# Splitting the 512-column products of the down and output projections into two of 256 columns

## The reference

```python
# first block, per layer
    x = x + jnp.einsum('bsnd,bsnd->bsd', gates, up) @ w_out[l]      # output projection, 1024 x 1024
    h = rmsnorm(x, norm_mlp_g[l])
    x = x + jnp.square(jax.nn.relu(h @ w_up[l])) @ w_down[l]        # 1024 -> 4096 -> 1024
...
# second block, per layer: two FFNs of this kind around a mixer
def _swiglu(x, w_in, w_out):
    gate, up = jnp.split(x @ w_in, 2, axis=-1)
    return (jax.nn.silu(gate) * up) @ w_out                         # 1024 -> 2 x 2816, 2816 -> 1024
...
        mixed = jnp.concatenate([o_a, o_b, o_c, o_d], axis=-1)
        h = h + g2[:, None, :] * (mixed @ w_out[l])                 # output projection, 1024 x 1024
```

## Time and profile before

| | |
|---|---|
| median of 3 runs | 2006.86 us (2004.92 to 2009.09) |
| the profiled execution | 2007.09 us, its span 2004.3 us |
| PE busy | 1952.3 us, 97% of the span, 13792 matmuls |
| PEld busy | 1761.0 us, 88%, 13792 loads |
| DVE busy | 1444.8 us, 72% |
| ACT busy | 1148.6 us, 57% |
| DMA | 409.55 MB, mean 204 GB/s |
| the chain that ended last | PE 79%, DVE 14%, ACT 5%, issue 2% |

### The profile page before, as it was taken

One profiled execution on the slowest core, in us unless ns is written; L12 is line 12 of the kernel. 1 busy time (PEld: TensorE's weight loads), 2 busy tenths in 40 slices (PEclk: granted clock), 3 DMA queues, 4 the chain that ended last, 5 costly groups with the idle time before them and its releaser, 6 DMA issues.

```text
span 2004.3 us, 33258 instructions
## 1 busy us (share of the span) xinstructions
PE 1952.3 (97%) x13792; PEld 1761.0 (88%) x13792; DVE 1444.8 (72%) x1922; ACT 1148.6 (57%) x1814; POOL 43.4 (2%) x32
## 2 busy tenths in 40 slices
PE   7999999999999999999899999999999999999999
PEld 7898888888989898888799988699989998878998
DVE  5756798888565788988756589765576657977555
ACT  6358845455436865454655566755565556566554
POOL 0100000000010000000000000000000100000000
PEclk9999999999999999999999999999999999999999
DMA  7453378996554356999455542365546554334553
GB/s 275 144 210 107 125 265 326 389 386 245 194 189 149 105 176 267 391 388 374 167 187 189 189 158 96 107 205 185 184 154 213 189 187 151 126 127 151 188 187 126
DMA packets 56164, 409.55 MB, mean 204 GB/s; under 512 B 6608, under 2 KB 6992, under 8 KB 7888
## 3 DMA queue, kind: packets, MB, share of 16 engines
q1 hardware_dynamic: 46512, 330.23, 46.5%
q10 hardware_dynamic: 9504, 77.21, 9.5%
HBM read 406.37 MB, written 1.05 MB: 203 GB/s over the span
## 4 chain that ended last, share of the span: by engine, by line
PE 79%; DVE 14%; ACT 5%; issue 2%; DMA 0%; DVEq 0%; ACTq 0%; SPq 0%
PE bank L603 25%; PE bank L605 24%; PE bank L604 24%; DVE weights_low L405 4%; ACT weights_high L383 1%; DVE work L2417 1%; DVE work L1517 1%; DVE scratch L1445 1%; ACT work L465 1%; PE bank L940 1%; DVE work L566 1%; DVE h_low L572 1%; ACT weights_high L384 0%; DVE work L1607 0%; DVE scratch L1602 0%
## 5 line engine op out<-in xcount | busy, mean ns | idle before, releaser
L405 DVE TENSOR_TENSOR weights_low<-raw_weights,weights_high 128x1024 fp32r<-128x1024 f32 x608 | 728.4, 1237 | 364.2 <-ACT weights_high L383 357.2
L603 PE MATMUL bank<-h_high,weights_high 128*128 128x256 f32 x3024 | 857.7, 284 | 15.0 <-DVE h_low L572 11.1
L605 PE MATMUL bank<-h_high,weights_low 128*128 128x256 f32 x3024 | 845.3, 280 | 0.0
L604 PE MATMUL bank<-h_low,weights_high 128*128 128x256 f32 x3024 | 844.7, 279 | 0.0
L383 ACT ACTIVATE weights_high<-raw_weights 128x1024 fp32r<-128x1024 f32 x296 | 313.4, 1059 | 619.6 <-PE bank L605 587.9
L603 PEld LDWEIGHTS bank<-h_high,weights_high 128*128 128x128 f32 x3024 | 567.9, 188 | 36.7 <-issue 17.0
L604 PEld LDWEIGHTS bank<-h_low,weights_high 128*128 128x128 f32 x3024 | 568.4, 188 | 2.9 <-issue 0.5
L605 PEld LDWEIGHTS bank<-h_high,weights_low 128*128 128x128 f32 x3024 | 568.6, 188 | 0.0
L384 ACT ACTIVATE weights_high<-raw_weights 128x1024 fp32r<-128x1024 f32 x296 | 309.0, 1044 | 0.0
L603 PE MATMUL bank<-weights_high,hidden_high 128*128 128x512 f32 x640 | 254.3, 397 | 5.1 <-DVE work L2491 2.9
L605 PE MATMUL bank<-weights_high,hidden_low 128*128 128x512 f32 x640 | 252.7, 395 | 0.0
(11 more groups left out here) (304 smaller groups left out, 1880.0 us busy)
## 6 DMA issues: line engine op xcount, KB each, us to landing
raw_weights<-in_stream SPq DMA_DIRECT2D x310, 1024.0 KB, 4.9
work<-in_ada ACTq DMA_DIRECT2D x64, 1152.0 KB, 9.4
consts<-in_consts SPq DMA_DIRECT2D x1, 2048.0 KB, 12.2
work<-in_row ACTq DMA_DIRECT2D x2, 836.0 KB, 5.5
x<-in_x SPq DMA_DIRECT2D x1, 1024.0 KB, 4.9
out_x<-x SPq DMA_DIRECT2D x4, 256.0 KB, 2.0
gain_row<-in_final SPq DMA_DIRECT2D x1, 512.0 KB, 12.8
vec<-in_vec SPq DMA_DIRECT2D x1, 169.0 KB, 12.1
```

The source lines that it names most:

```text
L405: dve.tensor_tensor(low[:, c], raw[:, c], high[:, c].bitcast(F32), ALU.subtract).then_inc(m.raw_done[plan.index[name] % RAW], 1)
L603: pe.matmul(out, aH, bH, start=start, stop=False, skip_group_check=True)
L604: pe.matmul(out, aH, bL, start=False, stop=False, skip_group_check=True)
L605: return pe.matmul(out, aL, bH, start=False, stop=stop, skip_group_check=True)
```

## The change

`three_wide` takes the place of `three` in `pe_down`, `pe_out` and `pe_mix`. It makes the three matmuls for the first 256 of the 512 columns, then the three for the other 256, with the same stationary tiles into the same bank. The flag that starts an accumulation is set on the first half alone. Every matmul loads its stationary tile as before. All waits and signals stay on the first and the last matmul of what was one triple. `T` is 256.

```diff
+def three_wide(pe, out, aH, aL, bH, bL, start, stop):
+
+    for c in (slice(0, T), slice(T, 2 * T)):
+        mm = three(pe, out[:, c], aH, aL, bH[:, c], bL[:, c], start and c.start == 0, stop)
+    return mm
...
@@ pe_down
-        return three(pe, m.ps[4 + 2 * tt + half][:, :], m.uH[:, at:at + P], m.uL[:, at:at + P], wH[:, c], wL[:, c],
-                     j == 0 and kt == 0, j == steps - 1 and kt == 1)
+        return three_wide(pe, m.ps[4 + 2 * tt + half][:, :], m.uH[:, at:at + P], m.uL[:, at:at + P], wH[:, c], wL[:, c],
+                          j == 0 and kt == 0, j == steps - 1 and kt == 1)
@@ pe_out
-            mm = three(pe, m.bank(plan, bank)[:, :], m.hH[:, at:at + P], m.hL[:, at:at + P], wH[:, c], wL[:, c],
-                       part == 0 and i == 0, part == 1 and i == 3)
+            mm = three_wide(pe, m.bank(plan, bank)[:, :], m.hH[:, at:at + P], m.hL[:, at:at + P], wH[:, c], wL[:, c],
+                            part == 0 and i == 0, part == 1 and i == 3)
@@ pe_mix
-        mm = three(pe, m.bank(plan, f"mo{i}")[:, :], high[:, at:at + P], low[:, at:at + P], wH[:, c], wL[:, c],
-                   n == 0 and kt == 0, n == 3 and kt == 1)
+        mm = three_wide(pe, m.bank(plan, f"mo{i}")[:, :], high[:, at:at + P], low[:, at:at + P], wH[:, c], wL[:, c],
+                        n == 0 and kt == 0, n == 3 and kt == 1)
```

## The result

The change takes 1993.41 us, the median of 6 runs (1989.74 to 1995.36), beside 2006.86 us for 6 runs of the kernel before (2002.86 to 2009.09). The ratio is 0.9929, 95% interval 0.9919 to 0.9939. The two medians alone give 0.9933, inside the interval. The profiled execution took 1995.36 us with a span of 1993.5 us.

A forecast was written before the change was run, and what follows sets the result against it. PE was taken as the bound: +2.7 us for split columns, less 0.2 us hidden in the mixer, nothing for loads, waits or the end, gave +2.5 us and a median of 2009.4 us; range for 8 in 10, 2002.5 to 2018.

The forecast's parts named there:

- What bounds the kernel: Whole kernel: TensorE is the bound, busy 97% of the span, at full granted clock in all 40 slices.
- the price of a product from start to start: FFN chunks: 233.3 ns for 512 columns, 117.7 ns for 256 usually, 113.3 ns at the fast pace.
- The term of the columns: Down and output projections: 2208 splits cost +4.6 us all slow, -14.8 us all fast; taken +2.7 us.
- their starts don't change: Second block's four FFNs: they read the slow pace and their starts stay, an argument against the fast-pace rival.
- The fast pace: Rival, FFNs: it spreads to up and gate products, 4.6 - 45 f us, 1998 us at three tenths; chance 0.14.
- A pace seems to be taken at the start of a stream and kept: Streams of 256-column products: each keeps its starting pace, 117.7 or 113.3 ns, the slow one far more usual.
- The loads: Split projections: 2208 more stationary loads of 0.19 us each, their price already in the 117.7 ns.
- The waits for the split: Heads of down and output chunks: first matmul keeps its waits; in an FFN none near enough to cost.
- the second rival: Down and output chunk heads: waits begin to cost, +5 us if a third do, +16 us if all; chance 0.17.
- the third: Rival, split triples: halves have their own price, 5 ns per pair, +11 us, pairs over 236 ns; chance 0.05.
- lost in the mixer: Second block's mixer, mc0 and mc1: 0.2 us of PE time hides behind the DVE and ACT chain.

The follow-up runs named there:

- experiment 9: Changed kernel plus, behind its last sum on an idle core, streams alternating activations past weights and weights past activations, then other widths: 2102.97 us, single run.

## Why the prediction was wrong

**What bounds the kernel, and the price of a product from start to start: right.** PE is the bound, the granted clock is full throughout, both paces were seen and measured, and 97% of the changed kernel's 256-column starts lie at one of the two (14113 of 14544). The durations would have misled, as the text said: 281 ns for 256 columns in the new projections, 397 for 512.

**The term of the columns: wrong in the share.** The sum took the projections alone, with one stream in ten at the fast pace (+2.7 us). In the changed trace about half of the weights-moving starts are fast (2420, with 2510 slow), and these products came out 4.9 us cheaper. With half of the projections at each pace the sum's own figures would have given (4.6 - 14.8) / 2 = -5.1 us. The prices of the two ends were right; the weight was taken from streams whose surroundings the change removes.

**The step that failed: "their starts don't change".** With it the forecast put the up and gate products, which the change doesn't touch, at nothing; they came out 9.8 us cheaper. The fast pace was a rival with a chance of 0.14, and with its term for the up and gate products it gave -9 us at a share of three tenths. What happened has about the size of this case, at -9.8 for the untouched products and -4.9 for the split ones, less 3.7 of new waits. It doesn't have its mechanism: the rival let an FFN keep the pace it started with, and that its 1998 us lies nearer to the result than the forecast does is partly luck. I argued against it that all FFNs of the second block started slow. A slow start doesn't matter, though: a down chunk of 256-column products as a rule turns a slow pace into the fast one (and the fast one into a slow one), as the streams of experiment 9 do with nothing else on the core. The trace before couldn't show this, since every down chunk had 512 columns and nothing else went from activations to weights in long 256-column streams. It did show the other half, that a wide chunk loses a fast pace. The stretch that the prediction read as 115.7 ns from a count (404 to 408) belongs to a fast up chunk, 113.3 from start to start behind its first; the up chunk behind the next down chunk is slow, 5.65 / 48 = 117.7:

```profile
402.81 0.38 PE L603 MATMUL bank<-h_high,weights_high 128*128 128x256 f32 x1
...
408.36 0.39 PE L603 MATMUL bank<-weights_high,hidden_high 128*128 128x512 f32 x1
...
413.95 0.28 PE L603 MATMUL bank<-h_high,weights_high 128*128 128x256 f32 x1
...
419.60 0.40 PE L603 MATMUL bank<-weights_high,hidden_high 128*128 128x512 f32 x1
```

"A pace seems to be taken at the start of a stream and kept" was half right: it is kept over chunk borders, waits for fulfilled semaphores and many matmuls, but mostly not over a change from activations to weights as the moving operand, nor over a wait that PE really sits through.

**Why the FFNs were slow before.** Gate and up products behind a wide product of weights past hidden come slow: the wide triple at 2034.23 with 117.8 behind it, and the run with the last triple wide. The kernel before has such a border behind 58 of its 76 down chunks (behind the others stand a further down chunk, other work or the end of the FFN), and the up or gate chunk is slow in all 58.

**The other parts held.** The loads cost nothing that shows in the pace (117.8 ns at most) though their cover shrank. The waits for the split cost 1.6 us more (5.0 for 3.4), where the second rival had +5 to +16, and a pair of halves takes at most 2 x 117.9 ns, under the 236 of the third. The rule of the Trainium skill ("TensorE: Matmul & The Clock Gate", "Back-to-back issue gap"), 2.5 ns more per split, would have given +5.5 us, an estimate: further off than the rows, since neither the rule nor the usual rows had the fast pace. That faster PE time is partly lost in the mixer was priced at 0.2 us; the waits there grew by 3.1.

**What stays open.** What in TensorE holds a stream at one of the two paces, why a wide product entered from a slow stream hands over the fast pace in most cases and not in all, and why a pause of PE mostly ends it. The paces were seen in one profiled execution of each kernel; the small spread of the runs suggests that they repeat.

## What to carry to other kernels

Read a matmul stream from start to start and per stretch, not by the mean duration, and look whether identical products run at two paces. If they do, the slow share is a reserve, and what stands just ahead of a stream can decide it. Here one 512-column matmul at the head of each down chunk and the rest at 256 gives 1981.4 us, ratio 0.9872, better than both kernels, with the same products computed. When a change makes neighbouring streams alike in form, price the untouched ones too.

## What the runs showed of the hardware

- TensorE runs streams of split-precision products of 256 columns with a load each at 117.8 or 113.3 ns, at the full granted clock, on the same operands.
- The pace as a rule alternates at the change from activations past weights to weights past activations, on an idle core too. In the changed trace slow became fast in 35 of 44 cases (not at 383.46 us, for one) and fast became slow in 28 of 28. On the way back it was kept in 50 of 50 cases without a pause, and a fast pace was lost in 6 of 7 with one.
- Activations past weights behind 512 columns of weights past hidden were slow in 58 of 58 cases, in the kernel before and in the run with the last triple wide.
- At the slower pace a product of 256 to 512 columns costs 0.451 to 0.460 ns per column. At 192 and 128 columns it is near 111.7 ns, whatever the width.
